# Gates behind the heads, and six pairs of gate panels in seven block products each

## The chip, the cores and the metric

The kernel runs on one core of one Trainium2 chip. The metric is the device time of one execution in microseconds (us), before and after the change. Engines are named as in the profile: PE is TensorE (matmuls, with PEld for its weight loads), DVE is VectorE, ACT is ScalarE, POOL is GpSimd, SP is SyncE, which issues most transfers.

## The reference

One layer of an encoder over 1024 tokens of width 1024, in float32. Cut to what matters:

```python
proj = u @ w_in                          # u = rmsnorm(x); 1024 x 5120
hc, bc, cc, q, k, v, gates = split(proj) # 512 each, gates 2 x 1024
y_conv = (bc * conv3(cc * hc)) @ w_conv_out            # z = bc * conv
# four heads of 128: two maps of 64 dims each, ALiBi bias
a = softmax(s1) - lam * softmax(s2)
o = rmsnorm(a @ v, subln_g) * (1 - lam_init)
y_attn = o @ w_attn_out
g = sigmoid(gates + b_gate)
merged = g[0] * y_conv + g[1] * y_attn
h = x + rmsnorm(merged @ w_o, g1)
out = h + rmsnorm(square(relu(rmsnorm(h, g2) @ w_ff1)) @ w_ff2, g3)
```

## The kernel before

Every float32 operand is split into a high part (rounded to the fp32r type, written by ScalarE as a copy) and a low part (VectorE: value minus high part), and a product is made of three matmuls: high x high, high x low and low x high (`PASSES`). A panel is 128 columns of a weight; a unit is one panel times one half (512) of the tokens, 8 row blocks x 3 passes = 24 matmuls of 128x512, into one bank of PSUM.

Each engine has its program written out by hand. The order in the heads comes from one list, `TURN`, which every engine's `walk` reads from left to right; each engine does its share of each word and waits by semaphores for the others. A word is a kind and a number. `q0 q1 k0 k1 v0 v1 h0 h1 c0 c1 b0 b1 g0 g1 g2 g3` are units (panel and half of the tokens; `g` are the gates). For block n of 128 queries, `Sn` are the scores of both maps on PE (8 matmuls, banks 2 to 5), `Xn` and `Mn` the addition of the bias and the maximum on DVE for the second and the first map (into e1 and e0), each with an exponential on ACT, `Cn` the joining of both maps into e0 (DVE, four operations), `Tn` the transposes of e0 on PE (8) with the high part on ACT, `TLn` their low part on DVE. `AV` is the product with v (24 matmuls), followed by a square on ACT and a copy on DVE; `O` the norm of its rows. A unit's second half also has the split of the panel after next: high part on ACT, low part on DVE (`split_lo`). The unit c1 has the convolution's three taps on DVE as well.

A turn of the loop is one head: block 7's end of the head before, and blocks 0 to 7. Two waits of PE and DVE carry what follows. PE waits ahead of `Sn` for `s_read`, which `M(n-1)` raises, since the scores use the same banks for every block:

```python
elif kind == "S":
    ...
    wait(pe, s_read, i * QB + n)
```

and DVE waits ahead of `Mn` until `T(n-1)` is done with e0:

```python
elif n > 0:
    dve.wait_ge(tb_done, tb_use(i, "T", n - 1) + 1)
```

`Xn` waits for `Sn` and for `C(n-1)`.

Gates: 16 panels of 128 columns. Each gate unit's tanh is made by ACT into one of two staging tiles and stored to DRAM, from where it comes back for the merge. Eight panels run inside the four head turns (four units a turn), four in the two lists of `AFTER` (with the last head's rest and the splits `ZS` and `OS` of z and o), and four in a loop behind them. Then come the branches (`z_hl`, `o_hl` times two weights, merged with the gates), w_o, the residual and norm, FF1 and FF2. FF1 is already made in pairs: from its third pair of panels on, a pair of panels times the tokens is seen as 2x2 blocks, and seven block products take the place of eight (`MIX_ORDER`: X1, Y, X2, Z1, X3, X4, Z2, 12 matmuls each), with sums of blocks of the tokens (`t_sum`, `t_lo`) made once ahead of them and sums of blocks of the weight for each pair.

Of the kernel before, what the change touches and what calls it, by code (L numbers as in the profile page):

```python
# [15 lines left out]

# [8 lines left out]
P = 128  # L25
# [35 lines left out]
def steps(text):  # L61
# [94 lines left out]
def unit_of(i, kind, n, after=False):  # L156


    if after:
        return i * (2 * GATE_PANELS) + (2 * HEADS * (len(PANELS) - 1) + n)  # L160
    return i * HEAD_UNITS + (2 * PANELS.index(kind) + n)


def panel_of(i, kind, n, after=False, ahead=0):


    per, first = (GATE_PANELS, HEADS * (len(PANELS) - 1)) if after else (HEAD_PANELS, PANELS.index(kind))
    j = first + n // 2 + ahead
    return i * per + j, j % RING, i * (per // RING) + j // RING
# [12 lines left out]
def build(nc, x, w_in, b_gate, conv_w, w_conv_out, lambda_qk, subln_g, w_attn_out, w_o, norm_g,  # L182
# [9 lines left out]
    with ctx:  # L192
# [14 lines left out]
        gate_bias = sb("gate_bias", [P, GATE_PANELS])  # L207
        small = sb("small", [P, 28])
# [13 lines left out]
        with ExitStack() as scope:  # L222
            z = sb("z", [P, CT, S], scope=scope)
            o = sb("o", [P, HEADS, S], scope=scope)
            with ExitStack() as loop_scope:
                table = sb("alibi", [P, 2 * S - P], scope=loop_scope)
                inner = sb("inner", [P, S + 2], scope=loop_scope)
                with ExitStack() as s1:
                    xn = sb("xn", [P, TT, D], scope=s1)
                    xsq = [sb(f"xsq{s}", [P, D], scope=s1) for s in range(2)]  # L230
                    par_rows = sb("par_rows", [NPAR, P], scope=s1)
                    lqk = sb("lqk", [P, 4, HD], scope=s1)
                    lq_junk = sb("lq_junk", [P, HD], scope=s1)
                with ExitStack() as s2:

                    q_st = [sb(f"q_stack{c}", [P, S], F32R, s2) for c in range(2)]
                    k_st = [sb(f"k_stack{c}", [P, S], F32R, s2) for c in range(2)]
                    k_lo = sb("k_lo", [P, S], F32R, s2)
                    v_hl = [sb("v_hi", [P, TT, P], F32R, s2), sb("v_lo", [P, TT, P], F32R, s2)]
                    e = [sb(f"e{c}", [P, S], scope=s2) for c in range(2)]  # L240
                    vt = e[1]
                    at_hl = [sb("at_hi", [P, TT, HALF], F32R, s2), sb("at_lo", [P, TT, HALF], F32R, s2)]
            with ExitStack() as s3:
                z_hl = [sb("z_hi", [P, CT, S], F32R, s3), sb("z_lo", [P, CT, S], F32R, s3)]
                o_hl = [sb("o_hi", [P, HEADS, S], F32R, s3), sb("o_lo", [P, HEADS, S], F32R, s3)]
# [1674 lines left out]
```

## Time and profile before

| | |
|---|---|
| median of 3 runs | 1437.19 us (1435.66 to 1437.87) |
| the profiled execution's own time | 1436.46 us |
| its span, first to last instruction | 1434.7 us |
| PE, DVE, ACT, POOL busy | 97%, 64%, 40%, 8% |
| mean granted PE clock | 0.994 of full |

The profile is of one execution. Busy shares are means over stages: a busy PE shows that it is fed, not that it is at its peak. A row of the timeline gives start and duration of an instruction; matmuls overlap, so the distance of two starts, not the duration, is what one costs. In brackets stands the idle time ahead of a row and what ended it.

### The profile page before, as it was taken

To read this page: it belongs to the slowest core of one execution; us is meant where nothing else is said; L and a number is where in the kernel's file an instruction comes from. 1 tells how busy PE (TensorE), PEld (TensorE's weight loads), DVE (VectorE), ACT (ScalarE), POOL (GpSimd) and SP (SyncE) were. 2 spreads that over 40 slices of the span, in tenths; PEclk is the share of its full clock that TensorE was granted. 3 is DMA by queue.
4 is the path that set the end of the run, shared out by engine and by line. 5 is a ranking of instruction groups with operands and counts; after the bars stand their busy time and mean duration, and the time that the engine had idled before them with its cause. 6 is when DMAs were issued, how large, how long until landed. Compare 5 with 4: busy or idle time off the path is not lost.

```text
span 1434.7 us, 17064 instructions
## 1 busy us (share of the span) xinstructions
PE 1394.5 (97%) x6281; PEld 1131.5 (79%) x6281; DVE 924.4 (64%) x1306; ACT 567.0 (40%) x871; POOL 111.3 (8%) x73
## 2 busy tenths in 40 slices
PE   5999999999999999999999999999999999999997
PEld 4877778777787777878788877888888877888886
DVE  6485576757657664156555698667774677775576
ACT  5434443533434454211233344333332444454453
POOL 0000000000000000000000143323333100000000
PEclk9999999999999999999999999999999999999999
DMA  5211111111111112344542155444444955336333
GB/s 166 59 30 59 42 33 60 44 29 44 58 29 29 58 66 74 103 154 143 192 165 72 44 169 161 143 152 161 161 147 148 387 199 170 102 97 226 95 111 132
DMA packets 141463, 161.96 MB, mean 113 GB/s; under 512 B 6813, under 2 KB 88922, under 8 KB 141274
## 3 DMA queue, kind: packets, MB, share of 16 engines
q1 hardware_dynamic: 135392, 148.40, 32.1%
q10 hardware_dynamic: 6010, 12.75, 2.3%
q8 instruction: 38, 0.62, 0.2%
q14 instruction: 23, 0.19, 0.0%
HBM read 114.98 MB, written 46.14 MB: 112 GB/s over the span
## 4 chain that ended last, share of the span: by engine, by line
PE 76%; DVE 10%; ACT 5%; issue 5%; DMA 4%; SPq 0%; ACTq 0%; DVEq 0%
PE psum L711 40%; PE psum L890 17%; PE psum L951 12%; DMA f_raw<-f_scratch 3%; PE psum L781 2%; PE psum L766 1%; PE psum L879 1%; DVE op L1749 1%; DVE v L1769 1%; PE psum L770 1%; DVE t_sum L1665 1%; DVE op L1752 1%; DVE v L1876 1%; ACT op L1253 1%; ACT w_hi L993 1%
## 5 line engine op out<-in xcount | busy, mean ns | idle before, releaser
L951 PE MATMUL psum<-op 128*128 128x512 f32 x1344 | 307.7, 390 | 2.9 <-DVE op L1752 2.6
L951 PEld LDWEIGHTS psum<-op 128*128 128x128 f32 x1344 | 251.4, 188 | 59.0 <-issue 4.4
L711 PE MATMUL psum<-act_hi,w_hi 128*128 128x512 f32 x640 | 257.8, 403 | 2.6 <-ACT staging L1059 2.3
L711 PE MATMUL psum<-act_hi,w_lo 128*128 128x512 f32 x640 | 250.4, 391 | 0.0
L711 PE MATMUL psum<-act_lo,w_hi 128*128 128x512 f32 x640 | 250.0, 391 | 0.0
L711 PEld LDWEIGHTS psum<-act_hi,w_hi 128*128 128x128 f32 x640 | 120.6, 188 | 31.7 <-issue 8.3
L711 PEld LDWEIGHTS psum<-act_hi,w_lo 128*128 128x128 f32 x640 | 120.5, 188 | 25.8
L711 PEld LDWEIGHTS psum<-act_lo,w_hi 128*128 128x128 f32 x640 | 120.8, 189 | 25.4 <-issue 1.9
L1749 DVE TENSOR_TENSOR op<-v,op 128x512 fp32r<-128x512 f32 x112 | 78.3, 699 | 71.1 <-ACT op L1253 71.1
L1396 DVE TENSOR_TENSOR w_lo<-w_raw,w_hi 128x1024 fp32r<-128x1024 f32 x52 | 65.1, 1252 | 82.0 <-ACT w_hi L993 80.2
L1253 ACT ACTIVATE op<-v 128x512 fp32r<-128x512 f32 x112 | 70.4, 628 | 118.2 <-DVE v L1769 69.1
L1070 ACT ACTIVATE e<-e,small 128x1024 f32<-128x1024 f32 x64 | 73.4, 1148 | 96.7 <-DVE small L1509 96.7
L1752 DVE TENSOR_TENSOR op<-f_raw,op 128x512 fp32r<-128x512 f32 x112 | 77.7, 694 | 33.0 <-ACT op L1255 33.0
L1504 DVE CUSTOM_DVE_ANT_0 e<-psum,alibi 128x1024 f32<-128x1024 f32 x64 | 78.1, 1221 | 21.9 <-issue 18.7
L1255 ACT ACTIVATE op<-f_raw 128x512 fp32r<-128x512 f32 x112 | 69.2, 618 | 46.1 <-DMA f_raw<-f_scratch 46.1
L993 ACT ACTIVATE w_hi<-w_raw 128x1024 fp32r<-128x1024 f32 x48 | 50.8, 1058 | 81.6 <-PE psum L711 72.7
L680 POOL TENSOR_TENSOR staging<-w_raw 128x512 f32<-128x512 f32 x1 | 1.3, 1297 | 812.8 <-ACT w_raw L1167 812.8
L1059 ACT ACTIVATE staging<-psum,gate_bias 128x512 f32<-128x512 f32 x32 | 22.0, 687 | 80.1 <-PE psum L711 77.4
L711 PE MATMUL psum<-wo_hi,act_hi 128*128 128x512 f32 x128 | 51.1, 399 | 2.0 <-DVE wo_lo L1601 2.0
L711 PE MATMUL psum<-wo_lo,act_hi 128*128 128x512 f32 x128 | 50.5, 395 | 0.0
L1389 DVE TENSOR_TENSOR at_lo<-psum,at_hi 128x1024 fp32r<-128x1024 f32 x32 | 39.1, 1223 | 17.6 <-ACT at_hi L1075 17.5
L711 PE MATMUL psum<-wo_hi,act_lo 128*128 128x512 f32 x128 | 50.4, 394 | 0.0
(218 smaller groups left out, 2470.2 us busy)
## 6 DMA issues: line engine op xcount, KB each, us to landing
f_raw<-f_scratch SPq DMA_DIRECT2D x112, 256.0 KB, 2.7
w_raw<-in_w_in SPq DMA_DIRECT2D x40, 512.0 KB
w_raw<-in_w_ff SPq DMA_DIRECT2D x32, 512.0 KB, 4.9
f_scratch<-f_out SPq DMA_DIRECT2D x56, 256.0 KB, 2.3
gates_scratch<-staging ACTq DMA_DIRECT2D x32, 256.0 KB, 2.0
gate_in<-gates_scratch SPq DMA_DIRECT2D x16, 512.0 KB, 4.2
v<-in_w_ff SPq DMA_DIRECT2D x8, 1024.0 KB, 7.9
v<-in_w_ff SPq DMA_DIRECT2D x4, 2048.0 KB, 10.4
```

What stands on the lines that cost most here:

```text
L711: mm = nc.tensor.matmul(bank, stat(a, kt), moving(b, kt), start=(n == 0), stop=(n == len(terms) - 1))
L890: mm = nc.tensor.matmul(bank, stat(a, kt), moving(b)[:, kt], start=(first and n == 0), stop=(last and n == len(terms) - 1), skip_group_che ...
L951: mm = nc.tensor.matmul(psum[:, (X_BANK, Z_BANK)[m % 2][t]], op[n % SLOTS][:, 2 + a, token_cols(t)], op[n % SLOTS][:, b], start=(m in (0, ...
L993: nc.scalar.activation(w_hl[slot][0][:], w_raw[slot][:], ACT.Copy).then_inc(w_hi, 1)
L1070: nc.scalar.activation(e[c][:], e[c][:], ACT.Exp, scale=SCALE, bias=neg_max[:, c:c + 1], accum_out=exp_sum[:, c:c + 1]).then_inc(exp_done, 1)
L1253: nc.scalar.activation(op[n % SLOTS][:, 0], v_block[m][:, kt], ACT.Copy).then_inc(v_hi, 1)
L1255: nc.scalar.activation(op[n % SLOTS][:, 2], f_raw[:, n % SLOTS], ACT.Copy).then_inc(f_hi, 1)
L1389: return vec.tensor_tensor(lo, src, hi, ALU.subtract).then_inc(semaphore, 1)
L1396: vec.tensor_tensor(w_hl[slot][1][:], w_raw[slot][:], w_hl[slot][0][:].bitcast(F32), ALU.subtract).then_inc(w_split, 1)
L1504: vec.tensor_tensor_reduce(out=e[c][:], in0=psum[:, SB + 2 * c:SB + 2 * c + 2].rearrange("p b c -> p (b c)"), in1=table[:, start:start + S ...
L1749: vec.tensor_tensor(slot[:, 1], v_block[m][:, kt], slot[:, 0].bitcast(F32), ALU.subtract).then_inc(v_split, 1)
L1752: vec.tensor_tensor(slot[:, 3], f_raw[:, n % SLOTS], slot[:, 2].bitcast(F32), ALU.subtract).then_inc(f_split, 1)
```

## The change

- The four gate units leave each head turn, which has twelve units now in place of sixteen. `TURN` is written anew: `S(n+1)` and `X(n+1)` stand ahead of the unit that they stood behind.
- Behind the heads, four gate panels run unit by unit (`AFTER`, banks 0 to 5, 0, 1) between the last head's rest, and DVE and ACT make the sums of the token blocks there.
- The other twelve run as six pairs in 2x2 blocks with the seven products of FF1's pairs, and the same four partial sums (three added on DVE, one read by ACT).
- Each block of a gate pair's weight has one buffer (high and low), refilled as soon as its product of the pair before is done, in the order `GATE_PARTS`.
- z and o are split into high parts laid out in the space of the head's tiles, under the last pair; the low parts have a place of their own.
- The branches use banks 0, 2, 4, 6 in place of 0 to 3. The loads of x for the residual wait for the merge's end.

```diff
-TURN = steps("C7 q0 O0 q1 T7 TL7 k0 AV1 k1 v0 O1 v1 S0 VT0 h0 X0 M0 C0 h1 S1 X1 T0 M1 TL0 C1 c0 S2 X2 T1 M2 "
-             "TL1 C2 c1 S3 X3 b0 T2 M3 TL2 C3 b1 S4 X4 g0 T3 M4 TL3 C4 g1 AV0 S5 X5 T4 M5 TL4 C5 g2 S6 X6 T5 "
-             "M6 TL5 C6 g3 S7 X7 T6 M7 TL6")
+TURN = steps("C7 q0 O0 q1 T7 TL7 k0 AV1 k1 v0 O1 v1 S0 VT0 h0 X0 M0 C0 S1 X1 h1 T0 M1 TL0 C1 S2 X2 c0 T1 M2 TL1 "
+             "C2 S3 X3 c1 T2 M3 TL2 C3 S4 X4 T3 b0 M4 TL3 C4 S5 X5 AV0 T4 M5 TL4 C5 S6 X6 b1 T5 M6 TL5 C6 S7 X7 "
+             "T6 M7 TL6")
...
-AFTER = [steps("C7 g0 O0 g1 T7 TL7 ZS0 g2 AV1 ZS1 g3 O1 ZS2"), steps("ZS3 OS0 g0 OS1 g1 OS2 g2 OS3 g3")]
+AFTER = steps("C7 g0 O0 g1 T7 TL7 g2 AV1 g3 g5 O1 g4 g7 g6")
+GATE_UNITS = [n for kind, n in AFTER if kind == "g"]
+GATE_BANKS = (0, 1, 2, 3, 4, 5, 0, 1)
...
+def pair_order(first, count, last_terms):
+    order, last = [], first + count - 1
+    for p in range(first, last):
+        order += [("X1", p)] + [("X4", p - 1)] * (p > first) + [("Y", p)] + [("Z2", p - 1)] * (p > first)
+        order += [("X2", p), ("Z1", p), ("X3", p)]
+    return order + [("X1", last), ("X4", last - 1), ("Z2", last - 1)] + [(x, last) for x in last_terms]
...
+GATE = Pairs(GATE_PANELS // 2, KT - GATE_PANELS // 2, ("X2", "Z1", "Y", "X3", "X4", "Z2"), (0, 0))
...
+TERM_BLOCK = {"X1": "W11", "Y": "W12", "X2": "S2", "Z1": "S3", "X3": "S1", "X4": "S4", "Z2": "W22"}
+GATE_PARTS = [(x, GATE.first) for x in ("W11", "W12", "S2", "S3", "S1")]
+for _p in range(GATE.first, GATE.end - 1):
+    GATE_PARTS += [("S1", _p)] * (_p > GATE.first)
+    GATE_PARTS += [("W11", _p + 1), ("S4", _p), ("W12", _p + 1), ("W22", _p), ("S2", _p + 1), ("S3", _p + 1)]
+GATE_PARTS += [(x, GATE.end - 1) for x in ("S1", "S4", "W22")]
...
+            first_use = {x: [(gate_ready, len(GATE_BANKS) - GATE_BANKS[::-1].index(b + s)) for s in range(2)]
+                         for x, b in (("X", 0), ("Y", 2), ("Z", 4))}
+            for kind, p in GATE.order:
+                pair_term(GATE, kind, p, first_use)
...
+            def g_part_hi(x, p):
+                ...
+                if p > GATE.first:
+                    act.wait_ge(mix_done, GATE.at(PART_TERM[x], p - 1))
+                ...
+                nc.scalar.activation(GATE.blocks(x, p)[0][:], gate_raw(x, p), ACT.Copy).then_inc(g_hi, 1)
```

Two places show how it moves instructions. The first is on PE in the first head, around the transposes of block 1 (T1). Before: the transposes, then the unit c1, from the third row on.

```order
L781 MATMUL psum<-ident,e 128x128 [waits tb_free,a_ready]
L781 MATMUL psum<-ident,e 128x128 x7
L711 MATMUL psum<-act_hi,w_hi 128x512 [waits h_ready]
L711 MATMUL psum<-act_lo,w_hi 128x512
L711 MATMUL psum<-act_hi,w_lo 128x512
```

Now, the same transposes, and behind them the scores of block 3 (k_stack and k_lo rows), which wait for `scores_read`, and only then the unit c1.

```order
L913 MATMUL psum<-ident,e0 128x128 [waits tb_free,a_ready]
L913 MATMUL psum<-ident,e0 128x128 x7
L898 MATMUL psum<-k_stack0,q_stack0 128x512 [waits scores_read]
L898 MATMUL psum<-k_stack0,q_stack0 128x512
L898 MATMUL psum<-k_stack1,q_stack1 128x512 x2
L902 MATMUL psum<-k_lo,q_stack0 128x512
L902 MATMUL psum<-k_lo,q_stack1 128x512
L902 MATMUL psum<-k_lo,q_stack0 128x512
L902 MATMUL psum<-k_lo,q_stack1 128x512
L838 MATMUL psum<-act_hi,w_hi0 128x512 [waits h_ready]
```

The scores' 8 matmuls moved from behind the unit to ahead of it, next to the transposes. So it is for blocks 2, 3, 4, 6 and 7; for blocks 4 and 7 the next transposes stand right behind the scores, without a unit.

The second is on DVE in the first head, from c1's product (`inner`) on. Before: the three taps and the low part of the next panel, then X3 (waits for the scores and C2), then b0's product.

```order
L1462 TENSOR_TENSOR inner<-psum,inner 128x512 [waits h_ready,proj_done]
L1470 TENSOR_SCALAR z<-inner,par 128x1024 [waits c_times_h_ready]
L1473 SCALAR_TENSOR_TENSOR z<-inner,par,z 128x1024 [waits conv_taps] x2
L1396 TENSOR_TENSOR w_lo<-w_raw,w_hi 128x1024 [waits w_hi_ready]
L1501 MEMSET small 128x1 [waits a_ready,scores_done]
L1504 ISA e,small<-psum,alibi 128x1024
```

Now, X3 first, then c1's operations, then M3, which waits for T2 and raises `scores_read`.

```order
L1709 MEMSET small 128x1 [waits a_ready,scores_done]
L1712 ISA e1,small<-psum,alibi 128x1024
L1712 ISA small 128x1
L1717 TENSOR_SCALAR small<-small 128x1 [waits map1_read]
L1674 TENSOR_TENSOR inner<-psum,inner 128x512 [waits h_ready,proj_done]
L1682 TENSOR_SCALAR z<-inner,par 128x1024 [waits c_times_h_ready]
L1685 SCALAR_TENSOR_TENSOR z<-inner,par,z 128x1024 [waits conv_taps] x2
L1608 TENSOR_TENSOR w_lo0<-w_raw0,w_hi0 128x1024 [waits w_hi_ready]
L1709 MEMSET small 128x1 [waits tb_done]
L1712 ISA e0,small<-psum,alibi 128x1024
L1712 ISA small 128x1
L1717 TENSOR_SCALAR small<-small 128x1 [waits scores_read]
```

c1's operations moved from ahead of X3 to between X3 and M3. In the same way h1's low part stands ahead of M1, b0's product ahead of M4 and b1's product and low part ahead of M6 now.

## Rows read from the trace of the kernel before

**Rows 1.** The page, its span and part 1: busy us, share, instructions.

```profile
span 1434.7 us, 17064 instructions
PE 1394.5 (97%) x6281; PEld 1131.5 (79%) x6281; DVE 924.4 (64%) x1306; ACT 567.0 (40%) x871; POOL 111.3 (8%) x73
```

**Rows 2.** Timeline of PE, first and last of 18 matmuls: start, duration, instruction.

```profile
149.83 0.39 PE L711 MATMUL psum<-act_hi,w_hi 128*128 128x512 f32 x1
...
153.68 0.39 PE L711 MATMUL psum<-act_hi,w_lo 128*128 128x512 f32 x1
```

**Rows 3.** Windows, one head turn: length, busy by engine, PEclk, DMA share, GB/s.

```profile
core 0: us, PE busy (x) PEld busy (x) DVE busy (x) ACT busy (x) POOL busy (x), PEclk, DMA share, GB/s
154.95:278.21 123.26, 122.43 (x573) 96.98 (x573) 83.26 (x137) 52.97 (x76) 0.00 (x0) 1.00 0.14 43
```

**Rows 4.** Timeline of PE, blocks 0 to 3 of the second head.

```profile
198.26 1.09 PE L781 MATMUL psum<-ident,e 128*128 128x128 f32 x8
199.10 0.48 PE L711 MATMUL psum<-act_hi,w_hi 128*128 128x512 f32 x1
...
204.67 1.08 PE L766 MATMUL psum<-k_stack,q_stack 128*128 128x512 f32 x4
...
206.88 1.09 PE L781 MATMUL psum<-ident,e 128*128 128x128 f32 x8 [0.46 <-DVE e L1521]
...
214.30 0.74 PE L770 MATMUL psum<-k_lo,q_stack 64*128 64x512 f32 x4
```

**Rows 5.** Timeline of DVE, X2 to X3 of the second head.

```profile
207.34 1.22 DVE L1504 CUSTOM_DVE_ANT_0 e<-psum,alibi 128x1024 f32<-128x1024 f32 x1
...
208.78 1.22 DVE L1504 CUSTOM_DVE_ANT_0 e<-psum,alibi 128x1024 f32<-128x1024 f32 x1
...
210.04 0.16 DVE L1509 TENSOR_SCALAR small<-small 128x1 f32<-128x1 f32 x1
210.98 1.22 DVE L1389 TENSOR_TENSOR at_lo<-psum,at_hi 128x1024 fp32r<-128x1024 f32 x1 [0.78 <-ACT at_hi L1075]
212.12 0.15 DVE L1515 RECIPROCAL small<-small 128x2 f32<-128x2 f32 x1
...
214.55 0.69 DVE L1462 TENSOR_TENSOR inner<-psum,inner 128x512 f32<-128x512 f32 x1
...
219.01 1.22 DVE L1396 TENSOR_TENSOR w_lo<-w_raw,w_hi 128x1024 fp32r<-128x1024 f32 x1
220.15 1.22 DVE L1504 CUSTOM_DVE_ANT_0 e<-psum,alibi 128x1024 f32<-128x1024 f32 x1
```

**Rows 6.** Timeline of ACT: h1's copy and split, and M2's exponential.

```profile
196.73 0.60 ACT L1051 ACTIVATE inner<-psum 128x512 f32<-128x512 f32 x1 [1.16 <-PE psum L711]
197.22 1.05 ACT L993 ACTIVATE w_hi<-w_raw 128x1024 fp32r<-128x1024 f32 x1
...
210.85 1.14 ACT L1070 ACTIVATE e<-e,small 128x1024 f32<-128x1024 f32 x1
```

**Rows 7.** Timeline of DVE, the copy of AV0's result.

```profile
246.89 0.69 DVE L1532 TENSOR_SCALAR o<-psum 128x512 f32 x1 [2.54 <-ACT dev L1079]
```

**Rows 8.** Windows, three stretches that begin with PE idle; columns as above.

```profile
552.98:558.60 5.62, 3.36 (x8) 2.72 (x9) 1.30 (x2) 4.59 (x6) 0.00 (x0) 0.70 0.21 82
699.87:705.45 5.58, 3.57 (x10) 2.84 (x10) 3.54 (x5) 0.00 (x0) 0.00 (x0) 0.69 0.45 156
859.27:869.15 9.88, 5.30 (x13) 4.19 (x14) 7.87 (x6) 5.60 (x7) 0.00 (x0) 0.66 0.36 98
```

**Rows 9.** Groups of DVE, shapes apart: count, busy us, mean ns, idle before.

```profile
L1537 DVE RECIPROCAL dev<-dev 128x512 f32<-128x512 f32 x8 | 26.8, 3353 | 9.9 <-ACT dev L1082 9.8
L1665 DVE TENSOR_TENSOR t_sum<-act_hi,t_sum 128x2048 f32<-128x2048 f32 x2 | 5.6, 2824 | 0.0
L1665 DVE TENSOR_TENSOR t_sum<-act_hi 128x2048 f32<-128x2048 f32 x2 | 4.6, 2292 | 0.1
```

More of the change, by code:

```diff
@@ new lines, with __post_init__, slot, n @@
+@dataclass
+class Pairs:
+    first: int
+    count: int
+    last_terms: tuple
+    earlier: tuple
+    raw: tuple = ()
+    blocks: object = None
+    t: dict = None
+    t_sums: dict = None
+    sums: tuple = ()
+    def __post_init__(self):
+        self.order = pair_order(self.first, self.count, self.last_terms)
+        self.base = sum(self.earlier)
+        self.end = self.first + self.count
+        self.terms = 7 * self.base
+    def slot(self, p):
+        return (p - self.first) % 2
+    def n(self, p):
+        return self.base + p - self.first
+    def at(self, kind, p):
+        return self.terms + self.order.index((kind, p)) + 1
+    def landed(self, p):
+        return 32 * (self.earlier[self.slot(p)] + (p - self.first) // 2 + 1)
+    def t_sum_at(self, n):
+        return (10 if self.base else 0) + {1: 3, 3: 6, 2: 8, 4: 10}[n]
+    def t_split_at(self, n):
+        return (4 if self.base else 0) + {3: 1, 2: 2, 1: 3, 4: 4}[n]
@@ L252, in build @@
             wo_hl = [[None] * NH, [None] * NH]
-            for h in range(NH):
+            for h in reversed(range(NH)):
                 for a in range(2):
@@ L800, in _, with mix @@
                 walk(i, TURN)
-            walk(HEADS, AFTER[0], True)
-            walk(HEADS + 1, AFTER[1], True)
-            pe.wait_ge(s_read, HEADS * QB)
+            walk(HEADS, AFTER, True)
+            def mix(bank, stat, moving, first, last):
+                terms = [(kt, a, b) for kt in range(KH) for a, b in PASSES]
+                for n, (kt, a, b) in enumerate(terms):
+                    mm = nc.tensor.matmul(bank, stat[a][:, kt], moving(b)[:, kt], start=(first and n == 0),
+                                          stop=(last and n == len(terms) - 1), skip_group_check=True)
+                mm.then_inc(mix_done, 1)
@@ new lines, in _ @@
+            for k in range(3):
+                t_sum(GATE, 3, k)
+            last_turn("AV1")
+            for k in range(2):
+                t_sum(GATE, 2, k)
+            last_turn("g3")
+            t_lo(GATE, 3)
+            t_sum(GATE, 4, 0)
+            t_lo(GATE, 2)
+            t_sum(GATE, 4, 1)
+            g_sum("S3", p)
+            g_sum("S1", p)
+            last_turn("O1")
+            for x in ("W11", "W12"):
+                g_part_lo(x, p)
+            for x in ("S2", "S4"):
+                g_sum(x, p)
```

652 lines of the change are left out of this document (415 added, 237 removed).

## The prediction

> **What bounds the kernel now.** I read the page first: TensorE is busy 1394.5 of 1434.7 us [rows 1], so only 40 us of its time is not matmul, and any term must show up either as matmul time or as new TensorE idle time. Next the timeline of TensorE gives prices. Full matmuls start every (153.68 - 149.83) / 17 = 0.2265 us [rows 2], so one unit (24 matmuls) is 5.44 us. The windows by turn show one head turn of 123.26 us with 122.43 us of TensorE busy, 83.26 of VectorE and 52.97 of ScalarE [rows 3]: 0.83 us of idle a turn. Last I read one attention block on the three engines (rows 4 to 6), because that is where the order changes.
>
> A block in the trace of before. T0 (the eight transposes) starts at 198.26, the unit c0 runs from 199.10, S2 (the scores of block 2) starts at 204.67 and T1 at 206.88 after a wait of 0.46 us for C1 [rows 4]. VectorE then does X2 at 207.34, M2 at 208.78, its small step at 210.04, TL1 at 210.98, C2 from 212.12 to 214.6 [rows 5]; ScalarE does the exponential of M2 at 210.85 [rows 6]. So from the start of X to the end of C takes 7.3 us, which the TensorE work of one unit, S and T (8.2 us) just covers. In this order every wait between S, M and T has a unit of 5.44 us lying over it. The reader is to see that margin: 0.9 us a block.
>
> **The change part by part.**
>
> Matmuls. Twelve gate panels were 12 x 2 x 24 = 576 matmuls; six pairs of seven products of 12 are 504. 72 x 0.2265 = **-16.3 us**. The other units, z and o are as many as before. Sixteen gate units, 87 us, leave the head turns and run behind them, which costs nothing in itself.
>
> The head turns. With four units fewer, the new order puts S(n+1) right behind T(n-1) on TensorE. But S(n+1) waits until M(n) has read the scores' banks, and M(n) waits until T(n-1) has read e0 (the two fences of the order show both waits). Before, a unit lay between T(n-1) and S(n+1). Now I walk one turn. Prices: T issues for 0.84 and ends after 1.09 us [rows 4], S takes 1.7; M takes 1.22, its small step is over 1.41 us after M's start, the exponential starts 2.07 us after M at the latest and C's reciprocal 1.27 us after that [rows 5, 6]; C takes 2.4 to 2.5 [rows 5]; an engine hands over in about 0.1 us (C2 to the next operation, T1 0.13 behind C1).
>
> 1. S3 and S6, the plain case: T's end + 0.1 + M's 1.25 + 0.13 against T's issue end: 1.6 each, 3.2.
> 2. S2: h1 now stands between X1 and M1 on VectorE and ScalarE, and X1 must wait for C0. The exponential of X1 ends 2.6 us after C0's end, so ScalarE takes h1's copy (0.6) and the next panel's high part (1.05) [rows 6] late, VectorE its low part (1.22), then M1: 4.7.
> 3. S4: c1 stands ahead of M3, and c1's operations on VectorE, from the product to the end of the low part, are 220.15 - 214.55 = 5.6 us [rows 5]. c1's end + 0.1 + 5.6 + M 1.25 + 0.13 - T 1.1: 6.0.
> 4. T3 and T6 stand right behind S4 and S7 and need C3 and C6: M's start + 1.45 (exponential) + 1.28 + 2.5 + 0.13 = 5.4, against S's end at 1.4 + 1.7 = 3.1: 2.3 each, 4.6.
> 5. S5: b0 (0.69) stands ahead of M4: 0.1 + 0.7 + 1.25 + 0.13: 2.2.
> 6. T4 now follows AV0 directly and needs the copy of its result; in the trace the copy starts at 246.89 [rows 7] and S5 lay over it: 1.5.
> 7. S7: b1's product and the low part of the next panel stand ahead of M6: 2.7. S1 behind h0 alone, for M0: 0.9.
>
> Sum: 3.2 + 4.7 + 6.0 + 4.6 + 2.2 + 1.5 + 2.7 + 0.9 = 25.8 us a turn. The turn becomes 122.43 - 21.76 + 25.8 = 126.5 us, longer than before although 21.8 us of matmuls left it. Over four turns the idle grows by 4 x (25.8 - 0.83) = **+99.9 us**.
>
> For item 3, the row shows it first: S3's last products start at 214.30 and are over at 215.04, yet X3 starts at 220.15, right behind c1's low part [rows 4, 5]: VectorE takes its instructions in the order written. The Trainium skill ("TensorE: Matmul & The Clock Gate", in the section on the array of 16 blocks of 32x32) says the same, that VectorE and ScalarE are strictly first in, first out. By that rule and row the sum stands; could M overtake what stands ahead of it, S2, S4, S7 and S5 would cost 1.6, 1.6, 1.6 and 0 and the sum would be 44 us less.
>
> The clock. The windows show that TensorE's granted clock went from full (2.4 GHz) to half (1.2 GHz) behind idle times of 2.3, 2.0 and 4.6 us: means of 0.70, 0.69 and 0.66 over the stretches [rows 8]. The first two cost about 1.7 us each (3.3 us at half speed), the third about 2.6. The turn with the wait of 0.46 us has 1.00 throughout [rows 3, 4]. The new turn has six idle times of 2.2 us or more; behind S4 and S7 the slower products lie partly in the waits of T3 and T6. So three to four fall on the path, at 1.7: 5 us a turn. **+20 us**; bounds 0 (no fall behind the shorter ones and all hidden) and 4 x 10.
>
> The stretch behind the heads. VectorE must do there, before the first pair: block sums of 2.3 to 2.8 us each, ten of them [rows 9], two reciprocals of 3.35 [rows 9], three weight sums, the two panels' low parts and W11's part, some 52 us with a wait for the last high part, while TensorE has eight units, AV1, T7 and O, 51.5 us. The first product X1 also waits until the gate that last used its bank is read, behind ScalarE's parts S2, S3, S1: 56.7, so 5.2 us. Steady pairs: 84 matmuls are 19.0 us of TensorE, against 7 low parts, 4 sums and 3 additions of 0.7 on VectorE (10 us) and 9 us of ScalarE: hidden, with six products (16 us) for each block's refill in its one buffer. At the last pair X3 and X4 are neighbours, with a copy between: 0.8, and 0.3 for Z2. The splits of z and o lie under the last pair: 0. A fall of the clock: 1.7. Together 8.6, with 0.6 for AV1 and X2. What goes: the gap at 552.98 with its half clock (2.3 + 1.7) [rows 8], and one of 1.0 before the branches. Net **+3.6**. Bounds: -4 (no new wait) and +12 (everything late by a half more). DMA issues: the same loads and stores; a pair's two panels of 512 KB in 19 us are no more than FF1's pairs take.
>
> Sum against the profiled execution's own 1436.46 (0.7 under the median, 1437.19): 1436.5 - 16.3 + 99.9 + 20 + 3.6 = 1543.7; to the median's level **1544 us**. A measurement of this kernel tells about 0.2% (3 us) from no change.
>
> **The rivals.**
>
> A. The new waits are hidden and TensorE stays the bound. That needs S(n+1) not to wait for M(n) behind T(n-1). For it: VectorE is busy only 83 of 123 us in a turn [rows 3], so throughput is there. Against: it is a chain, not a load, and both waits stand in the order. Time: 1437.2 - 16.3 + 0 to 3.6 = 1421 to 1425, faster by 1%. It decides only if the new idle time stays under 12.7 us in all, 0.4 us a block; the shortest link, M itself, is 1.22. Chance 0.05.
>
> B. The plain waits are there, but the unit's own work ahead of M costs nothing (it is done in time). 44 us less and fewer long idle times, so clock 8: 1544 - 44 - 12 = 1488. Against: X3's late start. Chance 0.07.
>
> C. The clock stays down for long stretches of the second half of each turn, since idle time comes at every block. From S2 to T6 some 60 us of matmul time would take up to twice as long, part of it inside waits: 20 to 30 us more a turn, 1600 to 1650. For it: the third fall lasted from 862 to 869, longer than the others. Against: units of 5.44 us stand between most waits, and full clock was back 3.3 us later in two of three cases. Chance 0.08.
>
> **How the numbers follow.** The forecast (waits as walked, clock falling for some) has 0.80; its own range comes from the clock's bounds (-20, +20) and 15% of the waits (15): 1510 to 1580. That holds the case and little else, so it is the range: B and most of C lie outside, and are the 2 in 10. Slower by over 0.2%: forecast, B and C, 0.95, less 0.02 for something unseen; within 0.2%: 0.02, a point between A and B; faster: 0.05.
>
> **What would show it.** Head turns of about 130 us from T7 to T7 (126 at full clock) in place of 123.3, with TensorE busy some 100 to 105 us in them; waits of the first score matmul for VectorE's maximum step, 28 of 0.9 to 6 us, and of transposes for C, 8 of 2.3; granted clock under 0.97 in the head stretch; VectorE busy as before. Behind the heads, a pair every 19 us and one wait of about 5 us ahead of the first X1. Wrong would be: a turn near 101 us (A), S4's wait at 1.6 (B), a clock of 0.8 over the turn (C).

## The result, and the profile of the changed kernel

The changed kernel takes **1564.64 us** (median of 4 runs, 1563.23 to 1565.53) against 1437.43 us for the kernel before, run beside it (median of 4, 1435.66 to 1437.87). The ratio is 1.0887, with a 95% interval of 1.0868 to 1.0905: 8.9% slower, 127.2 us. The forecast was 1544, with 1510 to 1580 as its range.

The page of the changed kernel, the lines that answer to [rows 1], and the granted clock in 40 slices:

```profile
span 1562.5 us, 17087 instructions
...
PE 1432.2 (92%) x6209; PEld 1142.3 (73%) x6209; DVE 999.9 (64%) x1385; ACT 598.5 (38%) x922; POOL 111.5 (7%) x73
...
PEclk9988998997899899999999999999999999999999
```

TensorE has 72 matmuls fewer and is busy 37.7 us longer: something makes a matmul take longer. Its idle time rose from 40 to 130 us. The 8s and 7s of the clock all lie in the first 14 slices (to 547 us), within the heads. Behind the heads every slice is at 0.9 or more; 625 to 664 us, where the gate pairs begin, has 0.92.

The windows by turn, of a turn from one S1 to the next, which answers to [rows 3]:

```profile
core 0: us, PE busy (x) PEld busy (x) DVE busy (x) ACT busy (x) POOL busy (x), PEclk, DMA share, GB/s
202.14:335.81 133.67, 111.40 (x476) 84.52 (x477) 81.53 (x134) 48.85 (x70) 0.00 (x0) 0.91 0.08 24
```

A turn has 97 matmul records fewer than before and is 10.4 us longer (the next one, 136.03 us, is 12.8 us longer; their mean is 134.9). VectorE and ScalarE have a little less to do than before (81.5 and 48.9 us of work against 83.3 and 53.0). The timeline of TensorE in this turn, its rows with a wait (in brackets: idle time before, and who ended it), which answers to [rows 4]:

```profile
202.14 1.20 PE L898 MATMUL psum<-k_stack,q_stack 128*128 128x512 f32 x4 [0.74 <-DVE small L1712]
215.04 2.08 PE L898 MATMUL psum<-k_stack,q_stack 128*128 128x512 f32 x4 [4.48 <-DVE small L1712]
226.19 1.21 PE L898 MATMUL psum<-k_stack,q_stack 128*128 128x512 f32 x4 [1.33 <-DVE small L1712]
240.80 2.07 PE L898 MATMUL psum<-k_stack,q_stack 128*128 128x512 f32 x4 [6.15 <-DVE small L1712]
245.01 1.96 PE L913 MATMUL psum<-ident,e 128*128 128x128 f32 x8 [0.99 <-DVE e L1729]
255.47 1.80 PE L898 MATMUL psum<-k_stack,q_stack 128*128 128x512 f32 x4 [2.03 <-DVE small L1712]
265.99 1.09 PE L913 MATMUL psum<-ident,e 128*128 128x128 f32 x8 [1.51 <-DVE o L1740]
268.41 1.19 PE L898 MATMUL psum<-k_stack,q_stack 128*128 128x512 f32 x4 [1.33 <-DVE small L1712]
279.50 1.92 PE L898 MATMUL psum<-k_stack,q_stack 128*128 128x512 f32 x4 [2.69 <-DVE small L1712]
```

These are S1, S2, S3, S4, T3, S5, T4, S6 and S7 (T6 follows at 283.60 with 1.02). The prediction had 0.9, 4.7, 1.6, 6.0, 2.3, 2.2, 1.5, 1.6, 2.7 and 2.3 for them. Together they are 22.3 us, all the idle time of the turn (133.67 - 111.40). The second column shows the clock: four score matmuls take 1.20 us at full speed and 2.08 behind the long waits. The turn's matmuls would need 122.43 - 21.76 = 100.7 us at full clock [rows 3] and are busy 111.4.

Why S4 waits 6.15 us is seen on VectorE ahead of it, to be read beside [rows 5]:

```profile
233.90 0.69 DVE L1674 TENSOR_TENSOR inner<-psum,inner 128x512 f32<-128x512 f32 x1 [2.15 <-PE psum L838]
...
235.72 1.28 DVE L1685 SCALAR_TENSOR_TENSOR z<-inner,par,z 128x1024 f32 x1 [0.16 <-DVE z L1682]
...
238.37 1.22 DVE L1608 TENSOR_TENSOR w_lo<-w_raw,w_hi 128x1024 fp32r<-128x1024 f32 x1
239.51 1.22 DVE L1712 CUSTOM_DVE_ANT_0 e<-psum,alibi 128x1024 f32<-128x1024 f32 x1
```

The work of c1 (233.90 to 239.51, 5.6 us) stands ahead of M3 (239.51), and S4 waits for M3. The gap of 2.3 us behind the heads, with half clock behind it, that the kernel before had at 552.98 (the first line of [rows 8]) is gone.

From the start to the last head's T7 the changed kernel takes 567.38 us, the kernel before 523.74, though 16 units (87.0 us) left this part: the heads lost 130.7 us. From T7 to the end it is 995.1 us against 911.0, with 312 matmuls more (70.7 us): 13.4 us lost. 130.7 + 13.4 - 16.3 for the 72 matmuls is the 127.8 us between the two spans.

### The profile page after: what moved, and what is told of

The parts are those of the page before. It is cut to its first block, busy times and chain, and to the rows that moved or that the text cites. A ratio compares the mean times of both kernels' runs of the same rounds, so it can differ in the third digit from the quotient of the medians.

```text
span 1562.5 us, 17087 instructions
## 1 busy us (share of the span) xinstructions
PE 1432.2 (92%) x6209; PEld 1142.3 (73%) x6209; DVE 999.9 (64%) x1385; ACT 598.5 (38%) x922; POOL 111.5 (7%) x73
## 4 chain that ended last, share of the span: by engine, by line
PE 70%; DVE 15%; issue 6%; ACT 4%; DMA 3%; SPq 0%; ACTq 0%; DVEq 0%
PE psum L838 28%; PE psum L940 22%; PE psum L1091 14%; PE psum L898 2%; DMA f_raw<-f_scratch 2%; DVE g_sum L1775 1%; PE psum L913 1%; PE psum L902 1%; DVE e L1729 1%; PE psum L1068 1%; DVE w_lo L1608 1%; DVE v L2072 1%; ACT e L1201 1%; DVE t_sum L1775 1%; DVE op L2052 1%
## 5 line engine op out<-in xcount | busy, mean ns | idle before, releaser
L1465 ACT ACTIVATE op<-v 128x512 fp32r<-128x512 f32 x112 | 70.4, 629 | 117.8 <-DVE v L2072 70.7
L898 PE MATMUL psum<-k_stack,q_stack 128*128 128x512 f32 x128 | 46.5, 494 | 73.2 <-DVE small L1712 73.2
L838 PEld LDWEIGHTS psum<-act_hi,w_hi 128*128 128x128 f32 x448 | 87.8, 196 | 27.0 <-issue 9.7
L838 PEld LDWEIGHTS psum<-act_lo,w_hi 128*128 128x128 f32 x448 | 87.3, 195 | 19.2 <-issue 1.9
L838 PEld LDWEIGHTS psum<-act_hi,w_lo 128*128 128x128 f32 x448 | 86.9, 194 | 19.4
L898 PEld LDWEIGHTS psum<-k_stack,q_stack 128*128 128x128 f32 x128 | 26.5, 226 | 85.2 <-DVE small L1712 80.9
L1608 DVE TENSOR_TENSOR w_lo<-w_raw,w_hi 128x1024 fp32r<-128x1024 f32 x40 | 50.4, 1259 | 34.1 <-ACT w_hi L1133 32.6
L1133 ACT ACTIVATE w_hi<-w_raw 128x1024 fp32r<-128x1024 f32 x36 | 38.0, 1055 | 60.9 <-PE psum L838 59.1
```

The lines of the kernel that those rows point to most:

```text
L838: mm = nc.tensor.matmul(bank, stat(a, kt), moving(b, kt), start=(n == 0), stop=(n == len(terms) - 1))
L898: nc.tensor.matmul(psum[:, SB + 2 * c + half], q_st[c][:, n * P:(n + 1) * P], k_st[c][:, half_cols[half]], start=True, stop=False)
L1133: nc.scalar.activation(w_hl[slot][0][:], w_raw[slot][:], ACT.Copy).then_inc(w_hi, 1)
L1465: nc.scalar.activation(op[n % SLOTS][:, 0], v_block[m][:, kt], ACT.Copy).then_inc(v_hi, 1)
L1608: vec.tensor_tensor(w_hl[slot][1][:], w_raw[slot][:], w_hl[slot][0][:].bitcast(F32), ALU.subtract).then_inc(w_split, 1)
```

## The experiments

Twelve kernels, in groups by question. Every ratio is to the kernel before on the same chip.

| kernel | median us | ratio to before, 95% | against the changed kernel |
|---|---|---|---|
| e_side | 1508.72 | 1.0492 to 1.0524 | -55.9 |
| e_order | 1508.11 | 1.0467 to 1.0511 | -56.5 |
| e_before_swap | 1508.68 | 1.0481 to 1.0517 | (before + 72.0) |
| e_warm | 1539.44 | 1.0702 to 1.0738 | -25.2 |
| e_spread | 1503.27 | 1.0446 to 1.0481 | -61.4 |
| e_fill | 1519.60 | 1.0568 to 1.0601 | -45.0 (e_order + 11.5) |
| e_copy | 1565.43 | 1.0882 to 1.0912 | +0.8 |
| e_pad | 1557.22 | 1.0834 to 1.0864 | -7.4 |
| e_before_shift | 1441.76 | 1.0024 to 1.0051 | (before + 5.3) |
| e_before_shift64 | 1440.77 | 1.0019 to 1.0044 | (before + 4.4) |
| e_all | 1497.38 | 1.0411 to 1.0446 | -67.3 |
| e_spread_pad | 1498.47 | 1.0417 to 1.0452 | -66.2 |

### Is it the order of the heads?

**e_side** leaves TensorE's list as it is and gives VectorE and ScalarE a list of their own:

```diff
+SIDE = steps("... C0 S1 X1 T0 M1 TL0 C1 h1 S2 X2 c0 T1 M2 TL1 C2 S3 X3 T2 M3 TL2 C3 c1 S4 X4 T3 M4 TL3 C4 b0 "
+             "S5 X5 AV0 T4 M5 TL4 C5 S6 X6 T5 M6 TL5 C6 b1 S7 X7 T6 M7 TL6")
-                walk(i, TURN)
+                walk(i, SIDE)
```

> The changed kernel with TensorE's order as it is, but in the heads VectorE and ScalarE take their share of the units h1, c1, b0, b1 one step later, behind the softmax work that TensorE's transpose or score group waits for. Theory (the order on the side engines makes part of the waits, as they serve the units first): the waits ahead of S2, S4 and S7 fall from 4.5, 6.2 and 2.7 us to about 1.4 us each and the wait ahead of S5 from 2.0 to 1.7, 9.4 us a turn, and with less time at half clock 3 us more: 12 turns less about 4, so about 1515 us. Rival: the waits are a matter of TensorE's order alone, since a score group follows at once on the transposes whose results it needs; they move from one block to the next, and the time stays within 8 us of 1564.6.

It took 1508.72 us. The waits of e_side, grouped (us in total, times, longest); in the changed kernel the first line reads 73.2, 27, 6.2:

```profile
PE psum L902 <- DVE small L1716: 31.2, 26, 1.6
PE psum L917 <- DVE e L1733: 17.8, 8, 2.3
```

S2, S4 and S7 wait 1.33 us, as the theory had it. 55.9 us of the loss, the clock's part in it included, came from VectorE and ScalarE serving a unit ahead of the maximum that TensorE is waiting for.

**e_order** puts the unit back between the transposes and the scores on all engines, with the gates still behind the heads:

```diff
-TURN = steps("... M0 C0 S1 X1 h1 T0 M1 TL0 C1 S2 X2 c0 T1 M2 TL1 C2 S3 X3 c1 T2 M3 TL2 C3 S4 X4 T3 b0 M4 TL3 C4 "
-             "S5 X5 AV0 T4 M5 TL4 C5 S6 X6 b1 T5 M6 TL5 C6 S7 X7 T6 M7 TL6")
+TURN = steps("... M0 C0 h1 S1 X1 T0 M1 TL0 C1 c0 S2 X2 T1 M2 TL1 C2 c1 S3 X3 b0 T2 M3 TL2 C3 b1 S4 X4 T3 M4 TL3 C4 "
+             "AV0 S5 X5 T4 M5 TL4 C5 S6 X6 T5 M6 TL5 C6 S7 X7 T6 M7 TL6")
```

> The changed kernel with the heads in the order of the kernel before on all three engines: the unit stands between a block's transposes and the next score group (T0, unit, S1, as before) and no longer behind the score group; the gate units stay out of the heads, as in the changed kernel, so that one or two places a turn have no unit. Theory: most of the heads' loss comes from the order (the score group asks for the reduced maxima at once, with nothing between): the waits fall to about 1.3 us at the places left without a unit and to under 0.5 us elsewhere, the clock stays at its full level, a turn takes about 110 us instead of 134.2, and the whole about 1564.6 - 4 x 24 = 1470 us. Rival: with four gate units gone from each turn the heads have too little work to fill the waits in any order, and other waits take over: a turn of 120 us or more, 1510 us or more (the version in which only VectorE and ScalarE changed their order took 1508.7).

1508.11 us: 56.5 us come back, not 95. The turn takes 119.29 us:

```profile
191.78:311.07 119.29, 106.46 (x477) 82.94 (x476) 80.88 (x134) 48.11 (x69) 0.00 (x0) 0.93 0.09 27
```

and TensorE's timeline shows where it still waits, nearly all of it in the second half of the turn, where no unit is left (AV0, S6, T5, S7, T6; the second row, S5, waits for nothing):

```profile
229.47 0.80 PE L838 MATMUL psum<-at_hi,v_hi 128*128 128x512 f32 x1 [4.60 <-DVE at_lo L1601]
...
237.16 1.08 PE L898 MATMUL psum<-k_stack,q_stack 128*128 128x512 f32 x4
...
241.67 1.20 PE L898 MATMUL psum<-k_stack,q_stack 128*128 128x512 f32 x4 [1.74 <-DVE small L1712]
246.37 1.09 PE L913 MATMUL psum<-ident,e 128*128 128x128 f32 x8 [2.84 <-DVE e L1729]
249.14 2.08 PE L898 MATMUL psum<-k_stack,q_stack 128*128 128x512 f32 x4 [1.68 <-DVE small L1712]
253.84 1.97 PE L913 MATMUL psum<-ident,e 128*128 128x128 f32 x8 [1.47 <-DVE e L1729]
```

So the rival of this run was nearer. The order is nearly half of the heads' loss: T7 of the last head comes at 507.31 instead of 567.38, 60.1 us. e_side, with TensorE's list untouched, brings it to 509.86, so that TensorE's own list is hardly a part of it; the order of the three engines against each other is. The other 70.6 us (507.31 + 87.0 - 523.74) are still there in the old order. In a turn they are 12.8 us of waits where there were 0.8, and matmuls that are busy 106.5 us where full clock needs 100.7: 12.0 + 5.8 = 17.8 us, four times over.

**e_before_swap** is the converse, in the kernel before with its 16 units a turn:

```diff
-TURN = steps("... M0 C0 h1 S1 X1 T0 M1 TL0 C1 c0 S2 X2 T1 M2 TL1 C2 c1 S3 X3 b0 T2 M3 TL2 C3 b1 S4 X4 g0 T3 ... "
+TURN = steps("... M0 C0 S1 X1 h1 T0 M1 TL0 C1 S2 X2 c0 T1 M2 TL1 C2 S3 X3 c1 b0 T2 M3 TL2 C3 S4 X4 b1 g0 T3 ... "
```

> The kernel before, with all 16 gate panels in the heads as they were, but each turn's score group S(n+1) moved ahead of the unit or units that stood between it and the transposes, which is the one thing that the changed kernel does to the order of the remaining work. Same instructions, same number of them. Theory: the order alone makes the waits (a score group asks at once for what VectorE makes from the group before; VectorE and ScalarE serve the units first): about 20 us a turn and the clock's fall on top, so 1437 + 80 to 100 = 1517 to 1537 us. Rival: with 16 units in a turn there is enough work everywhere and the order does not matter: within 15 us of 1437.

1508.68 us, 72.0 more than before; the expectation had 80 to 100. One turn, and the largest of the new waits:

```profile
351.17:493.15 141.98, 128.58 (x572) 99.44 (x572) 84.08 (x137) 54.00 (x76) 0.00 (x0) 0.96 0.12 37
```

```profile
PE psum L766 <- DVE small L1504: 46.4, 27, 4.5
```

Among TensorE's waits in the kernel before, down to those of 0.3 us in all, there is none of the scores for `small`. It and a new one of T4 (6.0 us) are most of the 72; the rest is the clock, since the same matmuls are busy 128.6 us in this turn and 122.4 before. So the order alone costs this much, with all 16 units in place.

### What does the clock cost?

**e_warm** adds useless matmuls in six of the ten waits, the four longest (S2, S4, S7, S5) and those of T3 and T6 (T4, S3 and S6 wait longer than these two and were left as they are):

```diff
+SPIN = {("S", 2): (17, 0, "h", 1), ("S", 4): (24, 0, "c", 1), ("T", 3): (6, 0, "c", 1),
+        ("S", 5): (7, 1, "c", 2), ("S", 7): (9, 0, "z", 1), ("T", 6): (6, 0, "z", 1)}
+                for _ in range(count):
+                    nc.tensor.matmul(psum[:, bank], act_hl[0][:, 0, 0:P], act_hl[0][:, 0, half_cols[0]], ...)
```

> The changed kernel with 69 useless matmuls (128x512, into a bank that the next unit overwrites) added in each turn, ahead of the six longest waits of TensorE, one for each 0.23 us of the wait or a little less: S2 17, S4 24, T3 6, S5 7, S7 9, T6 6. No result changes. Theory (after these waits TensorE runs at 1.2 GHz for 24 to 31 us of each turn, which costs 8 to 10 us, and what lets the clock fall is the idle time before): with the waits filled the granted clock stays at 1.00, a turn takes about 127 us instead of 134.2, and the whole 1564.6 - 4 x 7.5 = 1535 us, though TensorE does 62 us more work. Rival: the clock's fall costs nothing, since the half-clock stretches lie where TensorE would wait in any case: no gain, and what the useless matmuls overrun is added, 1565 to 1600 us.

1539.44 us: 276 matmuls more, 25.2 us less. A turn of e_warm:

```profile
196.53:323.95 127.42, 118.66 (x545) 91.42 (x546) 81.54 (x134) 48.87 (x70) 0.00 (x0) 1.00 0.09 25
```

The granted clock is 1.00 and the turn 127.4 us, where the prediction had 126.5 for full clock. Each of the six waits still has 0.4 to 0.8 us left, so the useless matmuls delayed nothing. This turn is 7.5 us under the mean of 134.9; over the four heads T7 comes at 542.09 instead of 567.38, so the fall of the clock is worth 25.3 us, 6.3 a turn. It was forecast at 5.

### What do the empty places cost?

**e_spread** puts the units where e_order waited, with AV0 behind S5:

```diff
+TURN = steps("... M0 C0 S1 X1 T0 M1 TL0 C1 h1 S2 X2 T1 M2 TL1 C2 c0 S3 X3 T2 M3 TL2 C3 c1 S4 X4 T3 M4 TL3 C4 S5 X5 "
+             "AV0 T4 M5 TL4 C5 b0 S6 X6 T5 M6 TL5 C6 b1 S7 X7 T6 M7 TL6")
```

> The changed kernel with a new order of the heads on all three engines: the unit between a block's transposes and the next score group, as before the change, but the units put where the version with the old order still waited (it took 1508.1 us and waited 1.7, 2.8, 1.7 and 1.5 us at the places left empty late in the turn, and 4.6 us ahead of AV0): h1, c0, c1, b0, b1 stand ahead of S2, S3, S4, S6, S7, and AV0 behind S5. Theory (every empty place costs its wait and, where some lie close together, the clock): waits are left at S1 (0.7), S5 (about 2), T5 or T6 (1 to 1.5) and nowhere over 2.1 us, the clock stays up, a turn takes about 108 us instead of 119.3, and the whole 1508 - 4 x 11 = 1464 us. Rival: with 14 units a turn VectorE's chain from scores to transposes sets the pace, and the waits only move: within 10 us of 1508.

1503.27 us, 4.8 less than e_order where 44 were hoped for (the two intervals of the ratio overlap): the theory fell, the waits only moved. TensorE in a turn of e_spread (T0, then S5):

```profile
191.81 1.97 PE L913 MATMUL psum<-ident,e 128*128 128x128 f32 x8 [4.40 <-DVE e L1729]
...
227.37 2.07 PE L898 MATMUL psum<-k_stack,q_stack 128*128 128x512 f32 x4 [7.12 <-DVE small L1712]
```

T0 now stands right behind S1 and waits for the softmax of block 0, and S5 stands right behind T3 and waits for M4, with c1's work and X4 ahead of M4. The turn is 119.5 us, as in e_order.

**e_fill** asks the question the other way round. It is e_order with useless work in the places where the kernel before had its gate units:

```diff
+SPIN = {("T", 3): 24, ("AV", 0): 24, ("S", 6): 24, ("S", 7): 24}
+            def spin(i, kind, n):
+                if (kind, n) in SPIN:
+                    pe.wait_ge(z_ready, i * 2 + 1)
+                    for _ in range(SPIN[kind, n]):
+                        nc.tensor.matmul(psum[:, 0], act_hl[0][:, 0, 0:P], act_hl[0][:, 0, half_cols[0]], ...)
```

> The version with the heads in the old order (1508.1 us, a turn of 119.3 us), with four groups of 24 useless matmuls (128x512, into a bank that the next unit overwrites) in each turn, at the places where the kernel before had its gate units: ahead of T3, AV0, S6 and S7. No result changes. TensorE gets 384 matmuls more, 87 us of work. Theory (in an empty place the next score group waits for VectorE anyway: blocks 6 and 7 are 7.5 us apart without a unit and were 8.1 us apart with one in the kernel before, so that a unit there costs 0.6 us and not 5.4): the turn goes from 119.3 to about 123.2 us, that of the kernel before, and the whole to 1508 + 16 = 1524 us; the granted clock of the heads is back at 1.00. Rival: TensorE's work adds up, 1508 + 87 less the 12.3 us of waits a turn at most: 1546 us or more.

1519.60 us, near the theory's 1524 and far from the rival's 1546. 384 matmuls, 87 us of TensorE's time, cost 11.5 us. A turn of e_fill:

```profile
196.75:319.26 122.51, 122.01 (x574) 97.07 (x572) 80.85 (x134) 48.33 (x69) 0.00 (x0) 1.00 0.09 26
```

and the scores of its blocks 5, 6 and 7, to be set beside those of e_order above (237.16, 241.67 and 249.14):

```profile
246.15 1.08 PE L907 MATMUL psum<-k_stack,q_stack 128*128 128x512 f32 x4
...
254.22 1.07 PE L907 MATMUL psum<-k_stack,q_stack 128*128 128x512 f32 x4
...
262.29 1.07 PE L907 MATMUL psum<-k_stack,q_stack 128*128 128x512 f32 x4
```

From S6 to S7 it is 8.07 us with a unit and 7.47 without: 0.60 for 5.44 us of work. One pair of blocks is not the whole, though. From S5 to S6 it is 8.07 against 4.51, and from S7 to the next turn's S0 e_fill is 5.0 us quicker (43.5 against 48.4), since neither a wait of T6 nor half clock follows S7. The turn tells it rightly: 122.51 against 119.29, 3.2 us for four units, 0.8 each. Of their 21.8 us, 12.3 filled waits (0.50 us idle in place of 12.83) and 6.2 came back because the other matmuls, at full clock, are busy 100.3 us in place of 106.5. So a unit costs 0.8 us there, the clock's part included, and 5.44 behind the heads. This is where the rest of the loss comes from: with the heads in the old order, the four gate units that left a turn made it 119.3 instead of 123.3 us, 4 us shorter, and cost 21.8 us behind.

### The stretch behind the heads

In the changed kernel X3 of the first gate pair waits 7.07 us, and the matmuls behind it start 0.43 us apart instead of 0.23 (half clock) until 631.0:

```profile
626.61 0.77 PE L940 MATMUL psum<-act_hi,g_S_hi 128*128 128x512 f32 x1 [7.07 <-DVE w_lo L1810]
627.18 0.63 PE L940 MATMUL psum<-act_lo,g_S_hi 128*128 128x512 f32 x1
627.60 0.63 PE L940 MATMUL psum<-act_hi,g_S_lo 128*128 128x512 f32 x1
```

The name of the releaser misleads. X3 needs ScalarE's copy of X2's result, and this copy (625.93) stands behind the second pair's W11, whose weights landed at 620.43:

```profile
620.43 0.63 ACT L1254 ACTIVATE w_hi<-g_raw 128x512 fp32r<-128x512 f32 x1 [6.71 <-DMA g_raw<-in_w_in]
...
625.93 0.58 ACT L1272 ACTIVATE prod<-psum 128x512 f32<-128x512 f32 x1
```

Their load was issued late, at 612.67, when the operand g_sum1, in whose memory they land (both begin at byte 188256), had been split (the last operation of it on VectorE is over at 612.6):

```profile
612.67 0.99 SPq L620 DMA_DIRECT2D g_raw<-in_w_in  x2
```

**e_copy** moves the copies ahead:

```diff
-            for p in range(GATE.first, GATE.end - 1):
-                if p > GATE.first:
+            p = GATE.first
+            x_copy(GATE, 1, p)
+            x_copy(GATE, 2, p)
+            g_part_hi("W11", p + 1)
...
```

> The changed kernel with one change in ScalarE's order behind the heads: its copies of the second and third block product of the first pair of gate panels stand ahead of the high part of the second pair's W11, which waits for that pair's weights. In the changed kernel TensorE waits 7.07 us ahead of the fourth matmul group of that pair, and then runs 6 us at half clock. Theory: the copies are late only because of their place behind that high part; the wait falls to about 0.3 us, and 6.8 us of wait with about 2 us of half clock go: 1555.5 to 1557.5 us. Rival 1: the weights' load, begun only when the first branch's operands free their memory, is late for what follows too, and the wait moves to the next pair: within 2 us of 1564.6. Rival 2: VectorE is late at the same place on its own: wait about 3 us, 1560.

1565.43 us, no gain. The wait at X3 is gone, and there is one of 5.73 us in the next pair:

```profile
644.17 0.77 PE L940 MATMUL psum<-act_hi,g_S_hi 128*128 128x512 f32 x1 [5.73 <-ACT prod L1272]
```

Rival 1 holds: the wait moves, so the place of the copies is not the cause. That the cause is the chain that begins with the late load fits the rows but is not shown: no version with an earlier load was run, as it needs another layout of the memory.

### Why do matmuls take longer?

Behind the heads nothing waits in long stretches, and yet TensorE does fewer matmuls there in the same time. The diff drops the small tile `gate_bias` and widens `small`, and so moves every tile behind them by 32 bytes. As the program places them, in the kernel before all the large tiles there, and the `act` and `w` tiles in front of them, begin at multiples of 128 bytes (`wo_hi0` 114560, `act_hi` 16512); in the changed kernel those behind begin 32 bytes short of one (147296), and `act` and `w` are where they were.

**e_pad** and **e_before_shift** change one number each:

```diff
-        small = sb("small", [P, 30])
+        small = sb("small", [P, 36])
```

```diff
-        small = sb("small", [P, 28])
+        small = sb("small", [P, 36])
```

> The changed kernel with one number different: the tile of small constants is 36 columns wide instead of 30, so that every SBUF tile behind it lies 32 bytes further on, at the same offset within 64 bytes as in the kernel before. No instruction changes. In the changed kernel's trace some 1250 matmuls (the z and output branches, the output projection, and the feed-forward ones whose moving and stationary tile differ in their address by 32 bytes within 64) start 233.3 ns apart where those of before start 226.7 ns apart. Theory: the place of the two operands relative to each other costs these 6.6 ns; 1250 x 6.6 ns = 8 us, so about 1556.5 us (0.5% faster than the changed kernel), and all matmuls start 226.7 ns apart again. Rival: the 6.6 ns come from what runs beside them (evictions, transfers, the clock), which stays: no difference, 1564.6 us, and 233.3 ns in the same places.

> The kernel before, with its tile of small constants 36 columns wide instead of 28: every SBUF tile behind it moves by 32 bytes. Nothing else changes. Theory of the operands' place: about 1104 matmuls (z and output branches 384, output projection 384, feed-forward 336) go from 226.7 to 233.3 ns, +7.3 us, so about 1444.7 us (0.5% slower than before). Rival: the place means nothing and the spacing comes from the changed order of work: 1437.4 us and 226.7 ns throughout.

e_pad took 1557.22 us, 7.4 less than the changed kernel, and e_before_shift 1441.76, 5.3 more than before (7.6 between the two profiled spans). The windows show 50 us in the middle of the two branches, in the order before, changed, e_pad, e_before_shift. They count the unit matmuls' line alone, so the columns are PE, PEld, PEclk, DMA share and GB/s; the number in brackets behind TensorE's 50.00 is that of its matmuls:

```profile
640.00:690.00 50.00, 50.00 (x223) 41.39 (x222) 1.00 0.49 151
```

```profile
750.00:800.00 50.00, 50.00 (x216) 40.26 (x215) 1.00 0.50 155
```

```profile
750.00:800.00 50.00, 50.00 (x222) 41.41 (x221) 1.00 0.47 145
```

```profile
640.00:690.00 50.00, 50.00 (x216) 40.16 (x215) 1.00 0.45 143
```

The clock is 1.00 and TensorE busy throughout in all four, and 223 and 222 matmuls stand against 216 and 216. Spacing measured start to start: 226.8 ns against 233.2 (changed) and 233.5 (e_before_shift). The same change of one number makes it appear in the one kernel and go from the other, so that it is the place of the tiles.

**e_before_shift64** (44 columns) tries the rule "same offset within 64 bytes":

> The kernel before, with its tile of small constants 44 columns wide instead of 28: every SBUF tile behind it moves by 64 bytes, where 36 columns moved them by 32 bytes and cost 5.3 us. Theory (what counts is whether the two operands of a matmul lie at the same offset within 64 bytes): 64 bytes change nothing, 1436.5 us, all matmuls 226.7 ns apart. Rival (any shift behind the small tile costs, through the distance to the operands in front of it, or through the wider tile): as with 32 bytes, 1441.8 us, or more.

1440.77 us: the rival holds, and the rule falls. With 64 bytes the feed-forward matmuls of act with the mixed weights still start 233.4 ns apart (226.8 before), the output projection 231.0 (227.0 before), and the branches 228.9 (226.8 before). What stands is narrower: in these three stretches, with both operands at multiples of 128 bytes, the spacing is 226.7 to 227.0 ns, and with one of them 32 bytes off it is 233.1 to 233.5. Where both operands were moved together by 32 bytes (the gates' g_t by g_S, 227.8 ns in the changed kernel, and 226.8 in e_pad) it hardly changes.

### Together

**e_all** is e_order with the 36 columns and e_copy's order; **e_spread_pad** is the same with e_spread's turn.

> The changed kernel with three things undone or changed together: the order of the heads as before, the SBUF tiles behind the small one at their old offset within 64 bytes, and ScalarE's copies of the first gate pair ahead of the second pair's W11. Measured alone the alignment gave 7.4 us and the copies nothing. Theory (the effects add): what the order alone gives, less 7.4 us: about 1462 us. What remains against the kernel before is then the empty places in the heads and the second gate pair's wait for its weights. Rival: the engine order of before with 14 units a turn makes TensorE the only bound, and the 72 fewer matmuls show: 1437 - 16 = 1421 us.

> The version above with the SBUF tiles behind the small one at their old offset within 64 bytes (measured alone: 7.4 us less) and ScalarE's copies of the first gate pair moved ahead (measured alone: nothing). Theory: 7 to 8 us less than the version above, about 1457 us. Rival: in an order without long waits the matmuls' 6.6 ns lie beside VectorE's work and don't show: as the version above.

1497.38 and 1498.47 us. e_all is 10.7 under e_order, e_spread_pad 4.8 under e_spread: around the 7.4 that the place of the tiles gives. Both expected levels, 1462 and 1457, were built on what e_order and e_spread were hoped to give, and missed with them. No version beats the kernel before; the best is still 61 us above it, most of which is the 70.6 us of the empty places less the 16.3 of the matmuls. A version that keeps the gate units in the heads and pairs only the eight panels that were behind them already was not run; by the price of a matmul it would save an estimated 4 x 12 x 0.2265 = 10.9 us.

## Why the prediction was right, and where its sizes were off

**The matmuls, -16.3.** 6281 against 6209 in the pages, 72 fewer. But the sentence that sixteen gate units "leave the head turns and run behind them, which costs nothing in itself" hid the main point. It was true in the sum, since the waits were added in the heads. e_fill shows what it means: work of this size was nearly free where these units stood (0.8 us each in a turn, 11.5 us for 384 matmuls in all), and costs 87 us where they went.

**The waits of a turn, 25.8.** Right, item by item, to within 0.3 us for eight of ten. The two others, T3 and T6, were 1.0 instead of 2.3, because S4 and S7 ahead of them run at half clock and so fill part of the wait: T3 starts 5.5 us after M3 (239.51 to 245.01), where the item had 5.4. At full clock e_warm gives the turn that was forecast (127.4; forecast 126.5), and a heads' loss of 542.09 + 87.0 - 523.74 = 105.4 us against 99.9. e_side confirms item 3: taking the units' work from ahead of M gave 55.9 us, where rival B had 44 (its items as listed add up to 43) and 12 for the clock. The Trainium skill ("TensorE: Matmul & The Clock Gate", the section on the array of 16 blocks of 32x32), by whose rule VectorE and ScalarE take their instructions strictly in order, agrees: in the changed kernel M3 starts only at 239.51, behind c1's low part, and with the units' work behind M in e_side the waits of S2, S4 and S7 fall from 4.48, 6.15 and 2.69 us to 1.33.

**The clock, +20.** The mechanism was right and the size too small: 6.3 us a turn by e_warm, 25.3 in all. The prediction took 1.7 us a fall, for three to four falls; in the trace of the turn six groups of scores and transposes have the duration of half clock (1.8 to 2.1 us), and TensorE is busy 10.7 us more than full clock would need; a part of this lies where it would have waited anyway.

**Behind the heads, +3.6.** Measured 13.4, outside the bound of +12. The forecast wait ahead of the first X1 (5.2) was 0.55 us. The wait came two terms later, at X3 (7.07 and about 2.3 of half clock). By the rows it begins with the load into g_sum1's memory, which the prediction had let pass ("a pair's two panels in 19 us are no more than FF1's pairs take"): it had counted bytes and not asked when the memory comes free. That the forecast had a wait of 5 us behind the heads at all was half luck: the one it named did not come, and another did. The other 6.4 us (995.1 against 988.7 in e_pad) are the tiles' 32 bytes, which no step of the prediction looked at; the diff's lines of `gate_bias` and `small` do it.

**The sum.** 119.9 forecast for the heads with the clock, 130.7 measured; 3.6 against 13.4 behind them. That is 20.6 us, the distance of 1544 from 1564.6: some 5.5 from the waits, 5.3 from the clock and 9.8 from behind the heads, all on the same side. Only inside the last did one error hide another, the wait at X1 that did not come. Rival A (TensorE stays the bound), B (plain waits alone, 1488; e_side comes nearest to it, at 1508.7) and C (the clock stays down) are excluded by the turn and its waits.

## What to carry to other kernels

Before moving TensorE's work out of a stretch, ask what a unit costs there: compare a whole turn with and without it, since two neighbouring blocks gave 0.6 or 3.6 us here, as one looked at one pair or the next. Where another engine's chain sets the pace the work is nearly free, and moved to a stretch that TensorE bounds it costs its full time, here 0.8 against 5.4 us; a saving of 1% in matmuls can't pay for that. When an order is changed, write beside each wait what stands ahead of its releaser on that engine, and change the lists of the other engines with it: this alone was worth 56 us here. And when a small tile comes or goes, look where the large ones behind it end up.

## What the runs showed of the hardware

- The place of the two operands in SBUF changes the spacing of 128x512 matmuls: about 226.8 ns with both at multiples of 128 bytes, 233.1 to 233.5 ns where one is moved by 32 bytes against the other, 229 to 233 with 64 bytes. It touches 384 matmuls of the branches, 384 of the output projection and 336 of the feed-forward part in both kernels, and 144 of the gates in the changed one; 1104 x 6.6 ns are 7.3 us. Why, and the exact rule, stays open.
- The clock fell to half behind waits of 2 to 7 us, and also where shorter ones followed each other closely: in e_order S7 runs at half clock (2.08 us for four matmuls) behind waits of 1.74, 2.84 and 1.68 us. In the changed kernel a wait of 1.33 us (S3) left it full, and so did T4's 1.51 with S6's 1.33 behind it; in e_side the same two waits (1.50 and 1.33) were followed by half clock (2.07 us). Adding 276 useless matmuls in such waits made the kernel 25 us faster, at a granted clock of 1.00 instead of 0.91 in the turn.
